# A PEER block on one core: the table u laid out in pairs of blocks and loaded two blocks at a time

## The reference: what is computed

```
q = (ht @ w_query).reshape(...)                     # 8 heads, two halves of 128
top 16 of h.keys1 and of h.keys2, top 16 of their sums -> expert = e1 * 128 + e2
g = softmax(top_s)
act = gelu(einsum('thkd,td->thk', u_tab[expert], ht))
return einsum('thk,thkd->td', g * act, v_tab[expert])
```

## Time and profile before

| | us |
|---|---|
| median of 3 runs | 1607.15 |
| the profiled execution | 1612.53 |
| its span | 1610.7 |
| TensorE busy | 1522.4 (95%) |
| VectorE busy | 1264.9 (79%) |
| GpSimd busy | 991.9 (62%) |
| ScalarE busy | 687.4 (43%) |
| DMA traffic | 438.91 MB, mean 272 GB/s |

### The profile page before, as it was taken

How to read it: one execution, slowest core, us unless ns; L and a number is a source line. 1 busy time by engine, 2 the same in 40 slices (tenths; PEclk the granted TensorE clock), 3 DMA queues, 4 the chain that set the end, 5 groups by cost and what they waited for, 6 DMA issues and landing times.

```text
span 1610.7 us, 21748 instructions
## 1 busy us (share of the span) xinstructions
PE 1522.4 (95%) x7951; PEld 1264.9 (79%) x7951; DVE 1264.9 (79%) x2000; ACT 687.4 (43%) x1273; POOL 991.9 (62%) x608
## 2 busy tenths in 40 slices
PE   6998898969999999999999999999999999999996
PEld 2345575438889999999999999998888778778885
DVE  6768831483799999968788886458989888899987
ACT  2031562123334343468787786343333333333332
POOL 3511000024337777777676787778988888889865
PEclk9999999989999999999999999999999999999998
DMA  9975217212316777788989989999999999999981
GB/s 368 331 216 53 30 38 256 72 61 84 105 63 234 269 273 262 255 289 325 359 339 373 345 336 382 391 337 374 375 380 369 371 364 385 374 368 371 372 282 65
DMA packets 217302, 438.91 MB, mean 272 GB/s; under 512 B 37220, under 2 KB 129892, under 8 KB 215404
## 3 DMA queue, kind: packets, MB, share of 16 engines
q1 hardware_dynamic: 179612, 302.44, 53.5%
q0 software_dynamic: 36864, 134.23, 22.8%
q10 hardware_dynamic: 720, 0.85, 0.2%
HBM read 379.66 MB, written 56.64 MB: 271 GB/s over the span
## 4 chain that ended last, share of the span: by engine, by line
PE 40%; DMA 16%; POOL 6%; ACT 6%; issue 4%; DVE 4%; SPq 1%; POOLq 0%; ACTq 0%; DVEq 0%
DMA u_raw<-in_peer_uT 8%; PE ps L1650 7%; PE ps L1651 7%; PE ps L1652 7%; DMA v_raw<-in_peer_v 5%; DMA a_in<-act_scr 4%; PE ps L1673 4%; POOL vl L1542 4%; PE ps L1674 4%; PE ps L1675 4%; ACT hot1h L1583 3%; PE ps L1328 2%; POOL ring L1530 2%; PE ps L1329 2%; PE ps L1330 2%
## 5 line engine op out<-in xcount | busy, mean ns | idle before, releaser
L1536 POOL TENSOR_TENSOR utl<-u_raw,uth 128x1024 fp32r<-128x1024 f32 x128 | 307.6, 2404 | 156.5 <-ACT uth L1555 156.0
L1650 PE MATMUL ps<-h2h,uth 128*128 128x384 f32 x1024 | 348.8, 341 | 3.8 <-POOL utl L1536 3.8
L1542 POOL TENSOR_TENSOR vl<-v_raw,vh 128x1024 fp32r<-128x1024 f32 x128 | 310.5, 2427 | 55.2 <-ACT vh L1555 53.5
L1652 PE MATMUL ps<-h2h,utl 128*128 128x384 f32 x1024 | 343.6, 336 | 0.0
L1651 PE MATMUL ps<-h2l,uth 128*128 128x384 f32 x1024 | 343.4, 335 | 0.0
L1673 PE MATMUL ps<-vh,wh 128*128 128x512 f32 x768 | 300.2, 391 | 4.1 <-DVE wl L1859 3.7
L1675 PE MATMUL ps<-vh,wl 128*128 128x512 f32 x768 | 298.9, 389 | 0.0
L1674 PE MATMUL ps<-vl,wh 128*128 128x512 f32 x768 | 298.9, 389 | 0.0
L1854 DVE TENSOR_TENSOR w_f<-a_in,g_in 128x384 f32<-128x384 f32 x128 | 208.6, 1631 | 51.9 <-DMA a_in<-act_scr 51.0
L1555 ACT ACTIVATE vh<-v_raw 128x1024 fp32r<-128x1024 f32 x128 | 135.4, 1058 | 192.1 <-DMA v_raw<-in_peer_v 162.6
L1650 PEld LDWEIGHTS ps<-h2h,uth 128*128 128x128 f32 x1024 | 193.3, 189 | 4.8 <-POOL utl L1536 4.0
(11 more groups left out here) (357 smaller groups left out, 2274.2 us busy)
## 6 DMA issues: line engine op xcount, KB each, us to landing
u_raw<-in_peer_uT SPq DMA_DIRECT2D x128, 512.0 KB, 7.0
v_raw<-in_peer_v SPq DMA_DIRECT2D x128, 512.0 KB, 9.7
w_ada<-in_w_ada SPq DMA_DIRECT2D x12, 2048.0 KB, 14.3
act_scr<-acts SPq DMA_DIRECT2D x64, 384.0 KB, 4.8
g_scr<-stage SPq DMA_DIRECT2D x12, 2048.0 KB, 10.2
g_in<-g_scr SPq DMA_DIRECT2D x32, 768.0 KB, 9.5
a_in<-act_scr SPq DMA_DIRECT2D x64, 384.0 KB, 9.9
w_q<-in_peer_w_query SPq DMA_DIRECT2D x8, 1024.0 KB, 5.5
```

The source lines that it names most:

```text
L1536: tt(k.utl[b % 3][:, :, :].rearrange(f3), k.u_raw[:, b % 4].rearrange(f3), k.uth[b % 3][:, :, :].bitcast(F32).rearrange(f3), ALU.subtract) ...
L1542: tt(k.vl[:, n % 4], k.v_raw[:, n % 4], k.vh[:, n % 4].bitcast(F32), ALU.subtract).then_inc(k.vl_done, 1)
L1650: mm(o, hi, k.h2h[:, kt, SP:T], start=(kt == 0), stop=False)
L1652: ins = mm(o, lo, k.h2h[:, kt, SP:T], start=False, stop=(kt == DK - 1))
```

## The change

The host lays u out in pairs of blocks: partition p of a pair holds 8 KB, the 4 KB of the even block and behind it the 4 KB of the odd one. One DMA brings a pair into two neighbouring buffers of `u_raw`. Two semaphores take the place of four; both blocks of a pair wait for the same one. SP issues the load of pair p, blocks 2p and 2p + 1, in the odd steps b = 2p - 3, where the load of block 2p + 1 stood. The load of block 2p stood in the step before.

```diff
-    k.s_u = [k.sem(f"s_u{i}") for i in range(4)]
+    k.s_u = [k.sem(f"s_u{i}") for i in range(2)]
...
-        for b in range(4):
-            sp.dma_start(k.u_raw[:, b], io["peer_uT"][b]).then_inc(k.s_u[b], 16)
+        for p in range(2):
+            sp.dma_start(k.u_raw[:, 2 * p:2 * p + 2], io["peer_uT"][p]).then_inc(k.s_u[p], 16)
...
-        def load_u(b):
-            sp.wait_ge(k.utl_done, b - 3)
-            sp.dma_start(k.u_raw[:, b % 4], io["peer_uT"][b]).then_inc(k.s_u[b % 4], 16)
+        def load_u(p):
+            sp.wait_ge(k.utl_done, 2 * p - 2)
+            sp.dma_start(k.u_raw[:, 2 * (p % 2):2 * (p % 2) + 2], io["peer_uT"][p]).then_inc(k.s_u[p % 2], 16)
...
-            if b + 4 < NBLK:
-                load_u(b + 4)
+            if b % 2 and b + 4 < NBLK:
+                load_u((b + 3) // 2)
...
-            act.wait_ge(k.s_u[b % 4], 16 * (b // 4 + 1))
+            act.wait_ge(k.s_u[b // 2 % 2], 16 * (b // 4 + 1))
...
-    return np.ascontiguousarray(u[0].reshape(PKEYS, PKEYS, DK, P).transpose(0, 3, 2, 1))
+    return np.ascontiguousarray(u[0].reshape(PKEYS // 2, 2, PKEYS, DK, P).transpose(0, 4, 1, 3, 2))
```

## The result

The changed kernel takes 1634.3 us (median of four runs, 1629.5 to 1637.87), before 1611.08 us (four runs, one more than the prediction had; 1606.96 to 1618.11). The ratio is 1.0133, with a 95% interval of 1.0104 to 1.0162, which is 21 us slower. The forecast was 1631 us, 1.5% slower. The profiled execution has a span of 1632.9 us against 1610.7. The 22 us more lie in phase one: from its first u matmul to its last TensorE takes 601.3 us before (467.4 to 1068.7) and 623.9 us in the changed kernel (471.1 to 1095.0).

What follows compares the result with a forecast made beforehand. TensorE is busy nearly throughout, so only its idle time or clock counts. Pair costs 36.8 - 18 (longer runs) + 5 (clock) = 24 us on 1612.53, 1636.5; with the runs' median 5.4 below the profiled one, 1631 us, range 1617 to 1650.

Steps and rivals of the forecast that it cites:

- quiet stretch: Blocks 4 to about 63: the first load has 1.4 us to spare and loses 1.2; cost 0.
- whole pairs: Busy stretch, both loads behind a 2 MB store: first block readable only when second lands, 2.7 x 8 = 21.5 us.
- parted pairs: Busy stretch, four places with a store between the two loads; now both stand behind it: 4.7, 4.7, 3.5, 2.4, sum 15.3 us.
- forecast, 4 KB runs: Busy stretch: whole and parted pairs' cost if both halves move as fast as now, 36.8 us.
- forecast, longer runs: Busy stretch: the 36.8 us of pair costs less 18 us for longer runs, before the clock term; 18.8 us.
- costs TensorE its full lateness: Busy stretch: TensorE's hand of about 2 us is used up, so loads later than now delay it fully.
- The longer runs: Busy stretch: 8 KB beside 4 KB gathers gets two thirds of bandwidth, 1.5 us earlier per pair, 12 x 1.5 = 18 us.
- The clock: Busy stretch: longer TensorE stops bring three more falls to 1.2 GHz, 5 us; between none and ten more (17 us).
- That nothing changes: Rival, within 1%: pairs get nearly the whole bandwidth, parted ones cost 10 us or less; 1607 to 1620; chance 0.31.
- Much slower: Rival: no sharing gain, a clock fall at most of twelve places, 36.8 + 17 = 54 us, 1661; chance 0.08.
- Faster: Rival: one 1 MB transfer replaces two, ending `u_raw` waits earlier; at most 17 us, 1590; chance 0.04 of over 1%.
- The lower end of the range: Full sharing of bandwidth by the pairs: +10 us, 1617.

Runs made afterwards that it cites:

- pair, 4 KB runs: The change (one DMA per pair) with u in the old layout, two 4 KB runs per partition; 1656.53 us, 1.0267 of the kernel before.
- landing alone: Kernel before, loads and order kept; ScalarE waits for both blocks of a pair before copying the first, except at four store-parted pairs; 1646.99 us, 1.0218.
- order alone: Kernel before, single loads kept, but both issued in the odd step with the wait that the pair has; 1617.66 us, 1.0039.

## Why the prediction was right

*The direction and the place* were right: the quiet stretch costs nothing, ScalarE's order passes the lateness on, and TensorE stops at the groups. The time, 1634.3 for 1631, is nearer than its terms deserve, and that closeness is luck. Counted place by place in the traces, TensorE's idle time against before (us) is as below; the stops for `utl` behind the last store count with the fourth parted pair.

| | eight whole pairs | four parted pairs | sum |
|---|---|---|---|
| forecast, 4 KB runs | 21.5 | 15.3 | 36.8 |
| pair, 4 KB runs | 15.6 | 10.8 | 26.5 |
| landing alone | 19.4 | 0.6 | 20.0 |
| order alone | -4.1 | 9.0 | 4.9 |
| forecast, longer runs | 9.5 | 9.3 | 18.8 |
| the change | 4.2 | 8.8 | 13.0 |

*The whole pairs* were put at 21.5 us with 4 KB runs. The landing rule alone shows 19.4, so the cost of waiting for the second block was sized well; with the order changed too it is 15.6. In the change itself they cost 4.2 in place of the 9.5 that the forecast leaves them, the largest miss among the idle terms. *The parted pairs* were put at 15.3 and cost 10.8. The step that failed there is "costs TensorE its full lateness". At the first parted place the wait of 6.42 us became 4.29 at TensorE, where before neither the first block's copy nor TensorE had waited: a place without a stop has the time in hand to use up first. At whole pairs where TensorE already stopped the step holds, as 1.2 us more at both in the place of the earlier trace rows.

*The longer runs* were put at 18 us on the ground of turns run by run. The packet counts show those turns, in three lengths of run. The gain in idle time is 13.5 us (26.5 to 13.0): 11.4 at the whole pairs, where 12 was forecast, and 2.0 at the parted ones, where it was 6. With the clock's part (19.0 to 10.9) it is 22, as the times say. Why the parted pairs gain so little is open. The prediction left open whether turns go by runs or by bytes, with the Trainium skill's rule ("DMA: Bandwidth & Descriptors", section on queues, rings and completion order) of turns by packet, a packet holding several descriptors. The trace agrees that the queues take turns, but not on their length: here a turn is one run, and the measurement decides.

*The clock* was put at 5 us, three more falls. It is 10.9 us, at seven places in place of two. In the changed kernel TensorE's stops of 4.3, 3.5, 3.5, 3.4, 3.3, 2.5 and 2.0 us each have a fall beside them, those of 1.8, 1.2 and 1.1 none; before, those of 2.3 and 2.0 had one, and the other eight, of 1.7 us and less, none. I had seen two falls in ten stops and taken it for chance, where the two were the longest ones. The term was half its size; the idle term, 18.8 forecast and 13.0 found, was too large by about as much. The errors cancelled.

*The rivals.* That nothing changes would have needed pairs landing 11 us after their issue behind a store; the twelve land after 11.6 to 15.2 us. At the two that land after 11.6 and 11.9 TensorE doesn't stop at all, so this rival holds for two places of twelve. "Much slower" asked for no gain of the longer runs and falls at most of the twelve places. There were seven falls, but the gain was there; without it, in the pair with 4 KB runs, the time is 1656.53. "Faster" rested on one transfer in place of two: with the stores out of the way, the pair is 0.9923 and single loads 0.9918, so a larger transfer gives nothing that shows beside the landing rule, as the overlap in the earlier trace rows had said. The rule of the Trainium skill (same page, section on measured bandwidth) of at least 1 MiB to a transfer brought no gain to these queued loads; what the page gives there, and its 2.0 us for each transfer, was measured on transfers that GpSimd issued, and these are SP's. The lower end of the range leaned on full sharing at +10 us, where its own terms, 36.8 - 35 + 5, give 7. Of what should show it, three signs were wrong: only five of the twelve waits for u lie between 5 and 7 us (the others from 2.8 to 7.7); ScalarE's waits for u were to grow to 80 us and stayed at 66, and TensorE's waits for `stage` copies were to be near 30 and are 20.8.

## What to carry to other kernels

Where loads sit in one queue, ask of a merged load what its first user waits for now, and what the queue puts ahead of it: the merged load is as late as its last part. Here moving a 2 MB store behind the next load or two was worth 0.8%. With the store left ahead of them, the merged load cost 2.7%, of which its longer runs gave 1.3% back. Before moving a store later, look who waits for its buffer, since a second waiter at the same point of an engine's order undoes the gain.

## What the runs showed of the hardware

Two DMA queues with work took turns on the engines by packets of one run each, so the length of a run sets the share: 0.35, 0.49 and 0.67 with runs of 2, 4 and 8 KB beside one of 4 KB.

Longer stops of TensorE are paid nearly twice: in the change 13.0 us more of them went with 10.9 us lost at 1.2 GHz, in the landing rule alone 20.0 with 14.6. It isn't so everywhere: in the order alone 4.9 us more idle time went with no more lost. In the ten traces no stop under 1.9 us in this stretch has a fall beside it, and every one over 3.8 us has; between them it is mixed, as in the order alone, where stops of 3.1 and 3.5 us have one and those of 2.2 and 3.7 none. In the kernel before with the stores behind the loads, with no stop between 740 and 1000, the granted clock is 1.00 throughout that stretch. That the stops cause the falls is argued from where they lie; no run held the stops fixed and changed the clock.
